# Turn of the hidden rows and down product, each one gate/up tile earlier in the steps of a mixture-of-experts loop

## The chip, the cores and the metric

The kernel runs on one core of a Trainium2 chip. The metric is the device time of one execution in microseconds (us); lower is better. TensorE multiplies matrices into accumulator banks, VectorE and ScalarE work on rows, GpSimd helps in the early stages, and SyncE (SP) issues most transfers. 16 DMA engines carry the data of the core.

## The reference

One decoder layer for 256 prompt rows and 8 sample rows, all in float32: projections, block-sparse attention, a memory attention, a short convolution, an output projection with LayerNorm, and then a mixture of experts with a second LayerNorm. The part that matters here is the mixture: each of the 264 rows goes to its top 4 of 32 experts.

```python
def expert_block(args):
    xb, e = args
    gu = xb @ w_gate_up[e] + b_gate_up[e]          # 1024 x 2048 weights
    g, u = jnp.split(gu, 2, axis=-1)
    g = jnp.minimum(g, SWIGLU_LIMIT)
    u = jnp.clip(u, -SWIGLU_LIMIT, SWIGLU_LIMIT)
    hid = (u + 1.0) * g * jax.nn.sigmoid(SWIGLU_ALPHA * g)
    return hid @ w_down[e] + b_down[e]             # 1024 x 1024 weights
```

The results are weighted by the router's softmax and summed per row.

## The kernel before

**Stages.** The first 340 us hold projections, attention, router and the making of a block table. From 341 us to about 1345 us the mixture runs; the last LayerNorm ends the kernel.

**Blocks and steps.** The rows of an expert are cut into blocks of 32 slots. With these inputs there are 51 blocks for 32 experts: 18 experts have one block, 10 have two, three have three and one has four (expert 5 is blocks 8 to 11, expert 6 is 12 to 14, expert 16 is 25 to 27, expert 23 is 37 to 39). Block i is worked on in step i of TensorE's loop (L952). A step multiplies the block's rows with eight gate/up tiles (`gate_up_tile`, L876), and in between does the second half of the block before it, d = i - 1: it turns that block's hidden rows (`turn_hidden`, L902, two transposes) and multiplies them with the four down tiles (`down`, L910). Odd steps (side 1) also gather the rows of the next pair of blocks after tile 4 and turn them after tile 5; even steps (side 0) instead add a finished pair into the sums after tile 5 (`add_pair`, L929).

**Weights.** One expert's weights are eight gate/up tiles and four down tiles of 1 MB each, and there is room for one expert only. SP's loop (L480) loads expert e: for each gate/up tile it waits until the last block of expert e - 1 has used it (`gu_used`, L483), issues the load, and then does the same with the four down tiles (`dn_used`, L487). All waits of SP stand in this one order, so a down tile's wait holds back the next expert's gate/up loads. TensorE waits for a gate/up tile at L878 and for a down tile at L920.

**Hidden rows.** After tile 7 VectorE takes four operations (`hidden`, L1819 to L1830) and ScalarE a sigmoid (L1203) to make the hidden rows of the block. `turn_hidden` waits for them (`hd_ready`, L904), ScalarE copies the turned rows (L1192), `down` waits for that copy (L912), and ScalarE copies its result (L1198). `down` first multiplies a bias row (L916), which releases VectorE's next bias row (`hot_used`).

**Expert numbers.** `pe.value_load` reads the number of the expert of block i (L960) and that of block d (L964) into registers; the waits at L878 and L920 use them.

Of the kernel before, what the change touches and what calls it, by code (L numbers as in the profile page):

```python
# [47 lines left out]
def layer_kernel(nc, x_prompt, x_sample, cache_k, cache_v, cache_mem_k, cache_mem_v, state_conv, page_table,  # L48
# [47 lines left out]
    with ctx:  # L96
# [405 lines left out]
        def _(pe):  # L502
# [343 lines left out]
            def gather(n):  # L846

                pe.wait_ge(hot_ready, n + 1)
                pe.wait_ge(rows_split, 1)
                for c in range(2):  # L850
                    for piece in range(3):
                        for half in range(2):
                            pe.matmul(p_gather[half * PAIR:(half + 1) * PAIR, :], slot_hot_b[:, c, :],  # L853
                                      x_pieces[c][piece][:, half * HALF:(half + 1) * HALF],
                                      start=(c == 0 and piece == 0), stop=False)
                for half in range(2):
                    last = pe.matmul(p_gather[half * PAIR:(half + 1) * PAIR, :], slot_hot_b[0:PACKED, 2, :],
                                     sample_packed[:, half * HALF:(half + 1) * HALF], start=False, stop=True)
                last.then_inc(gat_ready, 1)

            def turn_gathered(n):

                pe.wait_ge(gat_copied, n + 1)
                for j in range(4):
                    last = pe.transpose(p_gather[:, j * PARTS:(j + 1) * PARTS], xg[:, j * PARTS:(j + 1) * PARTS], ident[:, :])
                last.then_inc(xgt_ready, 1)

            def gate_up_bias(i, side):

                pe.wait_ge(bias_hot_ready, i + 1)  # L870
                for g in range(GROUPS):
                    pe.matmul(p_gu[side][g * SLOTS:(g + 1) * SLOTS, :], bias_hot[side].broadcast_to([3 * E, SLOTS]),
                              bias_up.rearrange("p (s n) -> p s n", s=2)[:, :, g * QUARTER:(g + 1) * QUARTER],
                              start=True, stop=False)

            def gate_up_tile(e, side, k):  # L876

                pe.wait_ge(gu_in[k], e * 16 + 16)  # L878
                for g in range(GROUPS):
                    last = pe.matmul(p_gu[side][g * SLOTS:(g + 1) * SLOTS, :],  # L880
                                     xg_t[:, k % 4, k // 4, side * SLOTS:(side + 1) * SLOTS],
                                     gate_up_w[:, k, :].rearrange("p (s n) -> p s n", s=2)[:, :, g * QUARTER:(g + 1) * QUARTER],
                                     start=False, stop=(k == KC - 1))
                last.then_inc(gu_used, 1)
# [17 lines left out]
            def turn_hidden(n):  # L902

                pe.wait_ge(hd_ready, n + 1)  # L904
                for r in range(2):
                    last = pe.transpose(p_hid_t[:, r * PARTS:(r + 1) * PARTS],  # L906
                                        hid.rearrange("p (c r) -> p r c", r=2)[:, r, :], ident[:, :])
                last.then_inc(hdt_ready, 1)

            def down(n, side, hot, e):  # L910

                pe.wait_ge(hdt_copied, n + 1)  # L912
                pe.wait_ge(dn_copied, 2 * n + 2)
                places = (0, PAIR) if side == 0 else (PAIR, 0)
                for h in range(2):
                    last = pe.matmul(p_down[places[h]:places[h] + SLOTS, :], hot.broadcast_to([3 * E, SLOTS]),  # L916
                                     bias_down[:, h * HALF:(h + 1) * HALF], start=True, stop=False)
                last.then_inc(hot_used, 1)
                for k in range(DK):
                    pe.wait_ge(dn_in[k], e * 16 + 16)  # L920
                    for h in range(2):
                        for r in range(2):
                            at_row = places[h] + r * SLOTS
                            last = pe.matmul(p_down[at_row:at_row + SLOTS, :], hid_t[:, r, k, :],  # L924
                                             down_rows[:, k, r, h * HALF:(h + 1) * HALF],
                                             start=(k == 0 and r == 1), stop=(k == DK - 1))
                    last.then_inc(dn_used, 1)

            def add_pair(pair, d, u):  # L929

                h, t = u // 4, u % 4
                if u == 0:
                    pe.wait_ge(weight_ready, pair + 1)
                if t == 0:
                    pe.wait_ge(dn_copied, 2 * d + (3 + h))
                pe.wait_ge(sum_added, 8 * pair + (u + 6))
                pe.matmul(bank[5 + u % 3][:, 0:T], pair_rows[:, h, t * PARTS:(t + 1) * PARTS], slot_weight_t[:, h, :],  # L937
                          start=True, stop=True).then_inc(sum_ready, 1)
# [13 lines left out]
            with pe.Fori(0, MAX_BLOCKS // 4) as group:  # L952
                for j, side in ((0, 1), (0, 0), (1, 1), (1, 0)):
                    q = group * 2 + j
                    i, d = group * 4 + (2 * j + 2 - side), group * 4 + (2 * j + 1 - side)
                    with pe.If(i < count):
                        pe.wait_ge(xgt_copied, i + 1)
                        pe.wait_ge(gu_read, i)
                        gate_up_bias(i, side)
                        e_up = pe.value_load(block_expert[0:1, bass.ds(i, 1)], min_val=0, max_val=E - 1)  # L960
                        for k in range(KC):
                            gate_up_tile(e_up, side, k)
                            if k == 1:
                                e_down = pe.value_load(block_expert[0:1, bass.ds(d, 1)], min_val=0, max_val=E - 1)  # L964
                            elif k == 2:
                                turn_hidden(d)
                            elif k == 3:
                                down(d, 1 - side, bias_hot[1 - side], e_down)
                            if side == 1:
                                if k == 4:  # L970
                                    gather(q + 1)
                                elif k == 5:
                                    turn_gathered(q + 1)
                            elif k == 5:
                                for u in range(8):
                                    add_pair(q, d, u)
                    with pe.Else():
                        pass
# [975 lines left out]
```

## Time and profile before

| | us |
|---|---|
| median of 3 runs | 1367.52 |
| range of the runs | 1364.51 to 1369.04 |
| the profiled execution | 1364.17 |
| its span on the core | 1362.4 |
| TensorE matmul busy | 1083.2 (80%) |
| VectorE busy | 612.0 (45%) |
| ScalarE busy | 231.4 (17%) |
| data moved | 499.39 MB, mean 367 GB/s |

Busy shares are averages over the span. TensorE's matmuls are pipelined and overlap in the records: the sum of their lengths is more than the time they take up, and the chain of waits shows the time that each adds. The releaser that a row names is the last one in the profile, which need not be what an engine stood for.

### The profile page before, as it was taken

The page shows a single profiled execution, that of the slowest core. Times are in us where ns is not written, and L with a number is a line of the kernel's source. Part 1 is how long each engine was busy: PE and PEld are TensorE (multiplying, and loading weights), DVE is VectorE, ACT ScalarE, POOL GpSimd, SP SyncE. Part 2 cuts the span into 40 slices and gives each one's busy share as a digit, 9 for nine tenths or more (in the row PEclk, how much of TensorE's full clock was granted, in tenths as well). Part 3 has the DMA queues.
Part 4 walks back from the last instruction along what each step waited for, and adds up shares of the span by engine and source line. Part 5 has one row for each costly group of instructions (what it writes and reads, how often), then busy time and mean ns, then how long its engine had stood idle before and what let it go on. Part 6 is the DMA issues. An engine that isn't in the chain of part 4 may idle for free.

```text
span 1362.4 us, 21271 instructions
## 1 busy us (share of the span) xinstructions
PE 1083.2 (80%) x7568; PEld 492.7 (36%) x7569; DVE 612.0 (45%) x1054; ACT 231.4 (17%) x505; POOL 154.9 (11%) x140
## 2 busy tenths in 40 slices
PE   7996757795997999976555569976969995869965
PEld 5775433232442344422212123422413441323423
DVE  1699865237644354533221215522534453324526
ACT  1211541113211111110000001211111111111112
POOL 2676722010600000000000000000000000000000
PEclk9999777897998999977877779977979997889988
DMA  9977949688899956699999999699999879999993
GB/s 368 374 309 286 397 156 366 267 316 335 362 409 421 422 237 272 260 421 422 421 422 421 422 423 421 270 422 422 422 422 421 367 324 422 422 422 421 423 422 132
DMA packets 72560, 499.39 MB, mean 367 GB/s; under 512 B 7459, under 2 KB 8022, under 8 KB 19190
## 3 DMA queue, kind: packets, MB, share of 16 engines
q1 hardware_dynamic: 66384, 430.14, 76.7%
q0 software_dynamic: 4816, 67.27, 12.4%
q10 hardware_dynamic: 1334, 1.64, 0.3%
q8 instruction: 16, 0.26, 0.1%
q14 instruction: 10, 0.08, 0.0%
HBM read 496.32 MB, written 2.71 MB: 366 GB/s over the span
## 4 chain that ended last, share of the span: by engine, by line
PE 45%; DMA 40%; DVE 7%; issue 4%; SPq 3%; POOL 1%; ACT 1%; ACTq 0%; DVEq 0%; POOLq 0%
DMA gate_up_w<-in_w_gate_up 23%; PE bank L880 15%; DMA down_w<-in_w_down 12%; PE bank L924 11%; PE bank L937 4%; PE bank L676 2%; PE bank L756 2%; DVE down_w L1484 2%; DMA gate_up_w<-in_w_out 2%; SPq L484 1%; PE bank L553 1%; DMA ring_b<-in_cache_k,page_row 1%; PE bank L906 1%; DMA ring_a<-in_cache_k,page_row 1%; PE bank L853 1%
## 5 line engine op out<-in xcount | busy, mean ns | idle before, releaser
L880 PE MATMUL bank<-gate_up_w,ring_b 128*32 128x512 f32 x3264 | 453.5, 654 | 178.0 <-DMA gate_up_w<-in_w_gate_up 177.7
L880 PEld LDWEIGHTS bank<-gate_up_w,ring_b 128*32 128x32 f32 x3264 | 102.0, 113 | 400.7 <-DMA gate_up_w<-in_w_gate_up 254.2
L924 PE MATMUL bank<-down_w,ring_b 128*32 128x512 f32 x1632 | 200.1, 598 | 10.5 <-DMA down_w<-in_w_down 10.5
L1812 DVE TENSOR_SCALAR work<-work 96x1 f32<-96x1 f32 x52 | 10.9, 209 | 325.4 <-PE bank L916 325.1
L1806 DVE TENSOR_TENSOR ring_a<-ring_a,bank 128x264 f32<-128x264 f32 x200 | 85.8, 429 | 138.7 <-PE bank L937 135.9
L924 PEld LDWEIGHTS bank<-down_w,ring_b 128*32 128x32 f32 x1632 | 89.3, 111 | 88.7 <-DMA down_w<-in_w_down 24.1
L1425 POOL TENSOR_TENSOR gate_up_w<-gate_up_w,ring_a 128x1024 f32<-128x1024 f32 x1 | 2.5, 2528 | 988.8 <-ACT gate_up_w L1238 988.8
L1198 ACT ACTIVATE ring_b<-bank 64x512 f32<-64x512 f32 x100 | 59.1, 591 | 240.2 <-PE bank L924 239.0
L937 PE MATMUL bank<-ring_b 128*128 128x264 f32 x400 | 95.7, 393 | 0.0
L937 PEld LDWEIGHTS bank<-ring_b 128*128 128x128 f32 x400 | 73.5, 189 | 32.8 <-issue 21.0
L1823 DVE TENSOR_SCALAR ring_b<-bank 128x256 f32<-128x256 f32 x51 | 21.6, 424 | 128.0 <-PE bank L880 128.0
L1192 ACT ACTIVATE ring_b<-bank 128x256 f32<-128x256 f32 x51 | 19.5, 383 | 336.7 <-PE bank L906 336.7
L1769 DVE SCALAR_TENSOR_TENSOR ring_a<-ring_a 128x1056 f32<-128x1056 f32 x50 | 66.7, 1334 | 0.9
L1772 DVE TENSOR_REDUCE ring_b<-ring_a 128x264 f32<-128x1056 f32 x50 | 62.6, 1253 | 1.7
L553 PE MATMUL bank<-x_cols,gate_up_w 128*128 128x264 f32 x256 | 61.0, 400 | 0.6 <-ACT x_cols L1043 0.6
L1203 ACT ACTIVATE ring_b<-ring_b 128x256 f32<-128x256 f32 x51 | 21.2, 416 | 223.8 <-DVE ring_b L1823 223.8
L553 PEld LDWEIGHTS bank<-x_cols,gate_up_w 128*128 128x128 f32 x256 | 49.9, 197 | 13.1 <-issue 2.3
L1484 DVE TENSOR_REDUCE down_w<-ring_b 128x32 f32<-128x2048 f32 x20 | 45.3, 2280 | 2.3 <-POOL ring_b L1322 2.1
L1478 DVE TENSOR_TENSOR ring_b<-ring_b,bank 128x2048 f32<-128x2048 f32 x12 | 27.3, 2279 | 38.3 <-ACT gate_up_w L1049 26.9
L1322 POOL TENSOR_TENSOR ring_b<-ring_b,gate_up_w 128x2048 f32<-128x2048 f32 x8 | 36.1, 4538 | 34.7 <-ACT gate_up_w L1049 26.7
L676 PE MATMUL bank<-gate_up_w,x_cols 128*128 128x512 f32 x64 | 30.6, 634 | 9.3 <-DMA gate_up_w<-in_w_out 9.3
L906 PEld LDWEIGHTS bank<-consts,ring_b 128*128 128x128 f32 x102 | 16.0, 206 | 57.1 <-issue 32.0
(367 smaller groups left out, 1082.1 us busy)
## 6 DMA issues: line engine op xcount, KB each, us to landing
gate_up_w<-in_w_gate_up SPq DMA_DIRECT2D x256, 1024.0 KB, 14.1
down_w<-in_w_down SPq DMA_DIRECT2D x128, 1024.0 KB, 11.4
gate_up_w<-in_w_in SPq DMA_DIRECT2D x4, 2048.0 KB, 19.7
gate_up_w<-in_w_out SPq DMA_DIRECT2D x1, 4096.0 KB, 23.9
ring_a<-in_w_in SPq DMA_DIRECT2D x1, 2048.0 KB, 24.9
ring_a<-in_w_mem_kv SPq DMA_DIRECT2D x1, 2048.0 KB, 28.1
gate_up_w<-in_cache_mem_k SPq DMA_DIRECT2D x1, 2048.0 KB, 15.3
gate_up_w<-in_cache_mem_v SPq DMA_DIRECT2D x1, 2048.0 KB, 20.3
```

The lines of the kernel that those rows point to most:

```text
L553: last = pe.matmul(out[:, 0:T], w, x_cols[:, k, :], start=(k == 0), stop=(k == KC - 1))
L676: last = pe.matmul(banks[half][0:rows, :], o_cols[:, j, c * PARTS:c * PARTS + rows], w_o[:, j, half * HALF:(half + 1) * HALF], start=(j == ...
L880: last = pe.matmul(p_gu[side][g * SLOTS:(g + 1) * SLOTS, :], xg_t[:, k % 4, k // 4, side * SLOTS:(side + 1) * SLOTS], gate_up_w[:, k, :].r ...
L906: last = pe.transpose(p_hid_t[:, r * PARTS:(r + 1) * PARTS], hid.rearrange("p (c r) -> p r c", r=2)[:, r, :], ident[:, :])
L924: last = pe.matmul(p_down[at_row:at_row + SLOTS, :], hid_t[:, r, k, :], down_rows[:, k, r, h * HALF:(h + 1) * HALF], start=(k == 0 and r = ...
L937: pe.matmul(bank[5 + u % 3][:, 0:T], pair_rows[:, h, t * PARTS:(t + 1) * PARTS], slot_weight_t[:, h, :], start=True, stop=True).then_inc(s ...
L1198: act.activation(pair_rows[at_row:at_row + PAIR, h, :], bank[1][at_row:at_row + PAIR, :], ACT.Copy)\
L1322: pool.tensor_tensor(pages, pages, q_wide[b % 4].unsqueeze(1).broadcast_to([PARTS, 4, AW]), ALU.mult)\
L1484: last = dve.tensor_reduce(scores[:, 4 * q:4 * q + 4, b * HEADS:(b + 1) * HEADS], page_quarter(b, q).rearrange("p (g h d) -> p g h d", g=4 ...
L1769: dve.scalar_tensor_tensor(weight_parts, token_slots, row_slots[:, h:h + 1], token_weights, ALU.is_equal, ALU.mult)\
L1772: return dve.tensor_reduce(slot_weight_t[:, h, :], weight_parts, AX.X, ALU.add)
L1806: dve.tensor_tensor(expert_sum[:, u, :], expert_sum[:, u, :], bank[5 + u % 3][:, 0:T], ALU.add)\
```

## The change

In each step the turn of the hidden rows moves from behind gate/up tile 2 to behind tile 1, the down product from behind tile 3 to behind tile 2, and the load of the down product's expert number from behind tile 1 to behind tile 0 (tiles are counted from 0). Nothing else is altered; what follows the last step (L979 on) stays as it is.

```diff
                         for k in range(KC):
                             gate_up_tile(e_up, side, k)
-                            if k == 1:
+                            if k == 0:
                                 e_down = pe.value_load(block_expert[0:1, bass.ds(d, 1)], min_val=0, max_val=E - 1)
+                            elif k == 1:
+                                turn_hidden(d)
                             elif k == 2:
-                                turn_hidden(d)
-                            elif k == 3:
                                 down(d, 1 - side, bias_hot[1 - side], e_down)
                             if side == 1:
                                 if k == 4:
```

## Rows read from the trace of the kernel before

**Rows 1.** Windows: stretch, its length, busy us (records) of each engine, TensorE clock, DMA share, GB/s

```profile
378.00:495.00 117.00, 104.22 (x836) 44.44 (x830) 49.73 (x102) 17.63 (x37) 0.00 (x0) 0.94 1.01 422
495.00:523.00 28.00, 27.45 (x230) 11.67 (x222) 14.90 (x30) 4.83 (x10) 0.00 (x0) 1.00 0.04 16
524.00:553.00 29.00, 29.00 (x250) 13.17 (x242) 14.90 (x30) 5.21 (x11) 0.00 (x0) 1.00 1.01 421
553.00:567.00 14.00, 14.00 (x130) 5.61 (x124) 9.29 (x15) 3.23 (x7) 0.00 (x0) 1.00 0.10 29
567.00:865.00 298.00, 205.50 (x1482) 76.65 (x1476) 89.98 (x183) 31.29 (x66) 0.00 (x0) 0.82 1.01 421
865.00:878.00 13.00, 12.61 (x98) 5.76 (x102) 5.04 (x12) 1.98 (x4) 0.00 (x0) 1.00 0.13 38
```

**Rows 2.** Chain of waits in a streaming stretch: start, us, what

```profile
608.74 3.51 PE bank L924 x29
615.77 20.93 DMA gate_up_w<-in_w_gate_up
638.01 3.50 PE bank L924 x30
```

**Rows 3.** Chain of waits around 498 us, where a gap begins

```profile
483.42 14.63 DMA down_w<-in_w_down
...
498.10 1.06 PE bank L924 x8
499.16 0.86 PE bank L880 x8
...
505.31 2.58 PE bank L880 x24
```

**Rows 4.** Timeline of TensorE: start, us, operation; idle time before it and what ended it

```profile
865.39 1.06 PE L924 MATMUL bank<-down_w,ring_b 128*32 128x512 f32 x8 [0.59 <-DMA down_w<-in_w_down]
1086.25 1.06 PE L924 MATMUL bank<-down_w,ring_b 128*32 128x512 f32 x8 [0.60 <-DMA down_w<-in_w_down]
```

**Rows 5.** Timeline of all engines in step 13: tiles 0 to 2, last hidden operation, turn

```profile
549.35 2.76 PE L880 MATMUL bank<-gate_up_w,ring_b 128*32 128x512 f32 x24
...
550.70 0.42 DVE L1830 TENSOR_TENSOR ring_b<-ring_b 128x256 f32<-128x256 f32 x1
...
552.03 0.31 PEld L906 LDWEIGHTS bank<-consts,ring_b 128*128 128x128 f32 x2 [0.84 <-DVE ring_b L1830]
```

**Rows 6.** Timeline: a VectorE result that TensorE stood waiting for

```profile
319.34 1.27 DVE L1587 SCALAR_TENSOR_TENSOR x_rows<-gate_up_w,small 8x1024 f32<-8x1024 f32 x1
...
320.66 0.57 PEld L688 LDWEIGHTS bank<-consts,x_rows 8*128 8x128 f32 x8 [0.78 <-DVE x_rows L1587]
```

**Rows 7.** Lines L960 and L964 in step 13: ends of the two register loads (ns, start us)

```profile
L960 PEldq SEQ_ASSERT  x1: 18/18/18, 549.0 to 549.0; - x1
L964 PEldq SEQ_ASSERT  x1: 18/18/18, 549.9 to 549.9; - x1
```

**Rows 8.** Timeline of SP: gate/up loads issued from step 11

```profile
521.58 2.04 SPq L484 DMA_DIRECT2D gate_up_w<-in_w_gate_up  x3
524.72 4.84 SPq L484 DMA_DIRECT2D gate_up_w<-in_w_gate_up  x2
```

**Rows 9.** Window: a hole in the stream in step 1

```profile
365.00:366.00 1.00, 1.00 (x15) 0.53 (x10) 1.00 (x1) 0.00 (x0) 0.03 (x1) 1.00 0.59 213
```

**Rows 10.** Chain of waits in the last step

```profile
1318.27 1.06 PE bank L880 x8
...
1319.54 3.45 PE bank L924 x32
1322.99 1.72 PE bank L880 x16
1324.70 3.76 PE bank L937 x16
```

**Rows 11.** Timeline: first gate/up tile of steps 6, 29 and 50 (of 16 such steps)

```profile
441.00 1.94 PE L880 MATMUL bank<-gate_up_w,ring_b 128*32 128x512 f32 x8 [9.89 <-DMA gate_up_w<-in_w_gate_up]
909.81 1.94 PE L880 MATMUL bank<-gate_up_w,ring_b 128*32 128x512 f32 x8 [6.80 <-DMA gate_up_w<-in_w_gate_up]
1310.80 1.94 PE L880 MATMUL bank<-gate_up_w,ring_b 128*32 128x512 f32 x8 [9.89 <-DMA gate_up_w<-in_w_gate_up]
```

## The prediction

> **What bounds the kernel now.** I read the page's slices first, then the windows, then the chain of waits, then single waits in the timeline.
>
> The windows split the expert part [rows 1] into two kinds of stretch. From 378 to 495, 524 to 553, 567 to 865 us and so on, the DMA engines are busy at a share of 1.01 and move 421 to 422 GB/s, whatever TensorE does (205.5 of 298 us busy in one of them). There the weight stream sets the time: 12 tiles per expert, each 1.049 MB / 422 GB/s = 2.48 us. In between lie four gaps in which almost nothing moves: 495 to 523, 553 to 567, 865 to 878, and 1086 to 1098 (not shown, same shape). These belong to the experts with three or four blocks (steps 8-11, 12-14, 25-27, 37-39): their weights stay in use until the last block, the next expert has nowhere to land, and TensorE is all but fully busy (27.45 of 28, 29.00 of 29, 14.00 of 14 us). So the run is: stream, plus gaps of TensorE work, plus a tail. Of the 51 steps, 16 wait 6.8 us or more for their first gate/up tile (first, shortest and last in [rows 11]); the other 35 run at TensorE's pace.
>
> The chain of waits in a streaming stretch [rows 2] reads "down product 3.5 us, then a gate/up transfer 20.9 us, then the down product": it looks as if every expert hung on the down product. It doesn't: that transfer is long because it queues behind others on busy DMA engines.
>
> How long a gap lasts is read from the chain at 498 us [rows 3]. The last down tile of the expert lands at 498.05; the last quarter of the down product (1.06 us), gate/up tile 4 (0.86 us), gather, tiles 5 to 7, the whole of step 10 and tile 0 of step 11 follow without a pause, and only then does SP issue the next gate/up tile, at 521.58 [rows 8]. The gaps at 865 and 1086 start the same way: TensorE stands 0.6 us before the last quarter of a down product until that tile lands [rows 4]. The gap at 553 has no landing in it: from 498 to 567 us TensorE waits for no transfer.
>
> **The change, part by part.** In each of 50 steps two transposes and the down product move ahead of one gate/up tile; the down product's four releases and SP's four down loads move with them, the load of the down product's expert number moves ahead of tile 1, and the release of tile 3 comes after the down product instead of before it. Nothing is added or removed. Steps of pure TensorE work keep their length if no new wait opens.
>
> 1. *Work behind the last landing.* In three gaps (498, 865, 1086) what lies between landing and release of the next expert's tile 0 is the path. The waiting instruction, the last quarter of the down product, has tile 3 in front of it now and behind it afterwards. One gate/up tile is 2.58 us / 3 = 0.86 us [rows 3]. The landing doesn't move, since the stream before it is full [rows 1]; TensorE just stands 0.6 + 0.86 us there. Cost 3 x 0.86 = **+2.6 us**. The gap at 553 is a chain of whole steps: no cost.
>
> 2. *Less cover for the turn.* The turn of the hidden rows starts at 552.03, behind tile 2 [rows 5]. Its input is done at 550.70 + 0.42 = 551.12. TensorE has loaded no weights for 0.84 us before it, but its matmuls run on: it waits for the array, not for VectorE, though the row names VectorE. Behind tile 1 it could start at 552.03 - 0.86 = 551.17. Another VectorE result (ends 320.61) let TensorE load at 320.66 [rows 6]: 0.05 us later. So the input is usable at 551.17 too: margin zero. No row shows this wait; its bounds are 0 and a whole tile, 0.86. It can't be below zero, because the array is busy until then. I take 0, by the nearest rows. Where it is on the path: between 498 and 564 us four turns (steps 10 to 13), none in the other two gaps. Sum 0, bounds 0 to +3.4 us. The copy of the turned rows keeps its cover: one tile lies between turn and product before and after.
>
> 3. *The expert number.* Its load ends at 549.9, that of the gate/up expert at 549.0 [rows 7], with tiles 0 and 1 handed out between. Handed out after tile 0 alone it ends about 549.8, while tile 1's matmul is due at 549.35 + 0.86 = 550.21. Hidden; 0 to 0.1 us in four steps.
>
> 4. *Tile 3 released late.* After a gap the stream starts from nothing, so each release counts. Tiles 0 to 2 feed it for 3 x 2.48 = 7.4 us, so tile 3 must be issued by 521.58 + 7.4 = 529.0. Before, the first tile behind the down product (tile 4) is issued at 529.2: two issues end at 524.72 + 4.84 = 529.56, and one takes 2.04 - 2 x 0.86 = 0.3 [rows 8]. Afterwards it is tile 3, one tile earlier, at 528.4. Margin 0.6 us, cost 0; if the start is ragged, up to 0.3 us in each of four gaps, **0 to +1.2**. Everywhere else down tiles queue ahead and cover it.
>
> 5. *Down tiles released earlier.* At full stream nothing is gained. The stream has small holes: at 365 us it drops to 213 of 422 GB/s for one microsecond [rows 9], because the first down reload is issued too late. The earlier product fills that, **-0.5 us at most**; the next gate/up loads are set by TensorE a few microseconds later, so I take 0.
>
> 6. *The tail.* In the last step tile 3 starts on its landing at 1318.27, product and tiles 4 and 5 follow, and the adds come at 1324.70 [rows 10]. Afterwards the product follows tile 2 and is over before tile 5 lands at 1318.27 + 2 x 2.48 = 1323.23; tile 5 takes 1.06 us like tile 3, and the adds come at 1324.3. **-0.4 us**.
>
> VectorE's and ScalarE's orders don't change; their work behind the product (bias row, slot weights, copies) only starts 0.86 us earlier.
>
> Of the clock: after 6.8 us or more of standing idle TensorE is granted the lower level, 1.2 GHz, and a tile takes 1.94 us [rows 11] instead of 1.06 [rows 10]. The product moves one tile nearer to those tiles and will run partly at 1.2 GHz in some of the 16 waiting steps. TensorE has over 6 us to spare there, so the sum doesn't change; only the last step could pay.
>
> The Trainium skill ("Perfetto Trace Analysis", Matmul Optimizations) says that the matmul engine scales its power with utilization and wants matmuls back to back in batches, which speaks against moving the product into a sparse stretch. By that rule the last step would pay up to a product's 3.45 us, by the rows nothing, since its tile 3 already ran in 1.06 us [rows 10].
>
> Sum: 2.6 + 0 + 0 + 0 + 0 - 0.4 = **+2.2 us**. The profiled execution took 1364.17 us (span 1362.4), which is 3.3 us under the median of the runs, 1367.52; so 1366.4 for an execution like it, and 1367.52 + 2.2 = **1369.7 us** for the median, +0.16%.
>
> **The rivals.**
> *The turn waits (slower).* If TensorE takes up a wait that isn't yet met later than 0.05 us, or the hidden rows come later, each turn at TensorE's pace costs w. Four lie on the path, and the two steps before each of the three landings first use up the 0.6 us of standing: total 2.2 + 4w + 3 x (2w - 0.6), the last term from w = 0.3 on. It passes 0.3% (4.1 us, about what a measurement of this kernel can tell from no change) from w = 0.37; at w = 0.5 it is +5.4 (1372.9), at w = 0.86 it is +9.0 (1376.5). For it: zero margin. Against: the 0.05 us of rows 6.
>
> *The chain is right (faster).* If the down reload's issue set the pace, as rows 2 read, it would come a tile landing (2.48 us) earlier in each of the 16 waiting steps: -40 us, 1328. Against it: a DMA share of 1.01 there leaves nothing to fill.
> The Trainium skill ("Perfetto Trace Analysis", Optimization Strategy) advises to find what the saturated engine waits for and make those dependencies start sooner, which is this rival's reasoning. It also gives 425 GB/s for large transfers and 435 for the fabric ("DMA: Bandwidth & Descriptors", Bandwidth); the trace's 422 agrees with a stream that is full.
>
> *Nothing moves (no change).* If the tile behind the landing is absorbed, because the stream recovers it from its own small holes, the time stays at 1367.5.
>
> **How the numbers follow.** Forecast 0.62, turn waits 0.20, nothing 0.12, chain right 0.06. The forecast lies 1.9 us below the 0.3% bound, and the three runs of before spread over 4.5 us, so 0.1 of its 0.62 would be measured as slower. Faster 0.06; same 0.52 + 0.12 = 0.64; slower 0.20 + 0.10 = 0.30. Range: below, the stream's holes filled and the spread of a median, 1365.5; above, late tiles of point 4 and w up to 0.6, about 1375.5. Outside are the chain rival and the far end of the turn's.
>
> **What would show it.** The waits before the last quarter of the down product near 498, 865 and 1086 us grow from 0.6 to 1.4 us, and the idle DMA stretches at the first, third and fourth gap each grow by 0.86 us, while the second keeps its length. The turn stands at 551.2 in a step like this one with hardly any TensorE idle time before it; if the waits list shows TensorE waiting for VectorE's last hidden operation in some 30 steps, the first rival holds. A DMA share under 0.95 within the first 10 us after a gap would mean point 4 was too kind. I am wrong if the streaming stretches move more than 422 GB/s, or if a gap changes by something other than one tile.

## The result and the profile after

| | before | after |
|---|---|---|
| median | 1364.83 us (20 runs, 1360.43 to 1382.15) | 1371.04 us (20 runs, 1366.86 to 1377.10) |
| ratio after / before | | 1.0039 (95% interval 1.0025 to 1.0054) |
| profiled execution, its span | 1364.17, 1362.4 us | 1371.56, 1369.8 us |

The change costs 0.39%, some 5.3 us. The ratio and its interval are of the fast runs alone, which leaves out one run of before (1382.15 us), and they are not the ratio of the two medians, which would be 1.0045. Timed a second time on another occasion it came to 1.0031 (1.0011 to 1.0050). The forecast was +2.2 us (+0.16%, range 1365.5 to 1375.5 us): the side of zero was right, the size was less than half of the 5.3 us. The absolute figure, 1369.7 us, lies only 1.3 us under the measured median, but by luck: it started from a median of three runs, 1367.52 us, which was 2.7 us above that of twenty. From 1364.83 us the same sum gives 1367.0 us, 4.0 us too low.

The windows after, cut where its stream stops and starts (columns as in rows 1):

```profile
378.00:495.00 117.00, 103.29 (x820) 43.92 (x816) 48.69 (x102) 16.85 (x35) 0.00 (x0) 0.94 1.01 420
499.00:525.00 26.00, 26.00 (x220) 12.33 (x216) 13.83 (x27) 4.84 (x10) 0.00 (x0) 1.00 0.00 0
528.00:556.00 28.00, 28.00 (x238) 13.02 (x233) 14.41 (x28) 5.22 (x11) 0.00 (x0) 1.00 1.00 406
559.00:569.00 10.00, 10.00 (x92) 3.26 (x88) 5.55 (x9) 2.86 (x6) 0.00 (x0) 1.00 0.04 7
572.00:869.00 297.00, 200.24 (x1460) 77.56 (x1452) 89.36 (x180) 31.33 (x66) 0.00 (x0) 0.82 1.01 420
870.00:882.00 12.00, 11.85 (x90) 5.40 (x94) 5.04 (x12) 1.78 (x4) 0.00 (x0) 1.00 0.04 5
```

The picture is that of [rows 1]: a full stream, and gaps in it while TensorE works. New is the third line: 406 GB/s after a gap, where [rows 1] had 421.

**A ruler for the stretches.** The early stages scatter: in thirteen profiles the first step starts anywhere from 337.2 to 344.0 us, though their code is the same in all. So I compare times inside the expert part, from one tile landing that TensorE waits for to another. These are the first gate/up tiles of steps 6, 16 and 29 after (timeline of TensorE); before they start at 441.00 and 909.81 [rows 11], and the middle one at 599.48.

```profile
442.66 1.94 PE L880 MATMUL bank<-gate_up_w,ring_b 128*32 128x512 f32 x8 [9.25 <-DMA gate_up_w<-in_w_gate_up]
604.11 1.94 PE L880 MATMUL bank<-gate_up_w,ring_b 128*32 128x512 f32 x8 [8.27 <-DMA gate_up_w<-in_w_gate_up]
917.28 1.08 PE L880 MATMUL bank<-gate_up_w,ring_b 128*32 128x512 f32 x4 [8.64 <-DMA gate_up_w<-in_w_gate_up]
```

With the first tiles of steps 41 and 50 (1139.36 and 1318.30 us after) and the end of the span this gives, in us, for the thirteen profiles:

| kernel | 6 to 16 (two gaps) | 16 to 29 (one) | 29 to 41 (one) | 41 to 50 (none) | 50 to the end | sum |
|---|---|---|---|---|---|---|
| before | 158.48 | 310.33 | 222.04 | 178.95 | 51.60 | 921.40 |
| before, again | 158.30 | 310.26 | 220.97 | 179.08 | 52.10 | 920.71 |
| the change | 161.45 | 313.17 | 222.08 | 178.94 | 51.50 | 927.14 |
| the change, again | 159.93 | 313.50 | 223.05 | 178.91 | 51.43 | 926.82 |
| turn only | 158.52 | 310.39 | 220.96 | 179.05 | 51.78 | 920.70 |
| tile 3 issued late | 160.34 | 311.91 | 221.38 | 178.90 | 51.71 | 924.24 |
| tile 3 issued later still | 160.75 | 313.19 | 224.11 | 179.06 | 51.52 | 928.63 |
| last quarter back | 158.30 | 310.26 | 221.04 | 178.90 | 51.57 | 920.07 |
| last quarter back, again | 158.28 | 310.54 | 221.06 | 178.98 | 50.86 | 919.72 |
| all one tile later | 159.42 | 309.46 | 220.14 | 179.11 | 53.45 | 921.58 |
| last quarter later | 158.32 | 309.58 | 219.91 | 179.08 | 52.76 | 919.65 |
| both splits | 158.46 | 309.58 | 220.26 | 179.11 | 52.51 | 919.92 |
| turn behind tile 0 | 165.21 | 313.30 | 224.87 | 178.86 | 52.10 | 934.34 |

The stretch without a gap is 178.9 to 179.1 us in every one of them, whatever TensorE's order: there the stream alone counts. Everything that the change costs lies in stretches with a gap, +1.5 to +3.1, +2.8 to +3.2 and, against 221.0, +1.1 to +2.1 us. The sums are 6.1 to 6.4 us above the repeat of before, and 5.4 to 5.7 us above its first profile. (The 222.04 of that first profile is its only value before step 50 that the second doesn't repeat; its restart at 1096 us took 1.2 us longer than the one in the repeat. That is chance, and about as large as some of the differences below.)

### The profile page after: what moved, and what is told of

Read it like the earlier page. It is cut to its first block, busy times and chain, and to the rows that moved or that the text cites. A ratio compares the mean times of both kernels' runs of the same rounds, so it can differ in the third digit from the quotient of the medians.

```text
span 1369.8 us, 21271 instructions
## 1 busy us (share of the span) xinstructions
PE 1083.0 (79%) x7568; PEld 502.0 (37%) x7569; DVE 611.3 (45%) x1054; ACT 231.7 (17%) x505; POOL 156.2 (11%) x140
## 3 DMA queue, kind: packets, MB, share of 16 engines
q0 software_dynamic: 4816, 67.27, 12.3%
## 4 chain that ended last, share of the span: by engine, by line
PE 47%; DMA 39%; DVE 6%; issue 4%; SPq 2%; POOL 1%; ACT 1%; DVEq 0%; ACTq 0%; POOLq 0%
DMA gate_up_w<-in_w_gate_up 22%; PE bank L880 16%; DMA down_w<-in_w_down 12%; PE bank L924 11%; PE bank L937 4%; PE bank L553 2%; PE bank L676 2%; PE bank L756 2%; DMA gate_up_w<-in_w_out 2%; DVE down_w L1484 2%; DMA ring_b<-in_cache_k,page_row 1%; PE bank L906 1%; DMA ring_a<-in_cache_k,page_row 1%; PE bank L853 1%; SPq L484 1%
## 5 line engine op out<-in xcount | busy, mean ns | idle before, releaser
L880 PE MATMUL bank<-gate_up_w,ring_b 128*32 128x512 f32 x3264 | 444.4, 643 | 182.9 <-DMA gate_up_w<-in_w_gate_up 182.6
L880 PEld LDWEIGHTS bank<-gate_up_w,ring_b 128*32 128x32 f32 x3264 | 108.6, 113 | 386.6 <-DMA gate_up_w<-in_w_gate_up 244.0
L924 PE MATMUL bank<-down_w,ring_b 128*32 128x512 f32 x1632 | 203.1, 603 | 15.4 <-DMA down_w<-in_w_down 15.4
## 6 DMA issues: line engine op xcount, KB each, us to landing
down_w<-in_w_down SPq DMA_DIRECT2D x128, 1024.0 KB, 12.5
gate_up_w<-in_w_out SPq DMA_DIRECT2D x1, 4096.0 KB, 23.5
ring_a<-in_w_in SPq DMA_DIRECT2D x1, 2048.0 KB, 25.8
```

Source lines behind the costliest of these rows:

```text
L880: last = pe.matmul(p_gu[side][g * SLOTS:(g + 1) * SLOTS, :], xg_t[:, k % 4, k // 4, side * SLOTS:(side + 1) * SLOTS], gate_up_w[:, k, :].r ...
```

## Where the time went

**One tile behind the last landing.** The chain after, at the third gap:

```profile
856.81 13.30 DMA down_w<-in_w_down
870.15 1.06 PE bank L924 x8
871.21 2.58 PE bank L880 x24
873.79 3.76 PE bank L937 x16
...
879.62 1.72 PE bank L880 x16
```

Behind the last down tile there are now three gate/up tiles (2.58 us) before the adds. From this landing, 870.11, to SP's issue of the next tile 0 at 880.7 are 10.6 us. Before it was 9.7 (865.34 to 875.1; below). The difference is the 0.86 us of the forecast. TensorE's standing before it did not grow to 1.4 us, as I had written (timeline of TensorE; [rows 4]):

```profile
870.15 1.06 PE L924 MATMUL bank<-down_w,ring_b 128*32 128x512 f32 x8 [0.59 <-DMA down_w<-in_w_down]
1093.77 1.06 PE L924 MATMUL bank<-down_w,ring_b 128*32 128x512 f32 x8 [0.59 <-DMA down_w<-in_w_down]
```

The tile that stands behind the landing one step pair earlier (24) had already made TensorE 0.86 us later, and the product came 0.86 us earlier in its step. The two cancel. Waits of 1.4 us stand elsewhere, in steps behind a streaming stretch (step 24 for one), before as after; the change puts a second wait in front of them (below).

**The restart.** I then followed the gate/up tiles that refill the buffer after this gap. SP's line L484 in narrow windows (last number of the first line: time of issue), with the time from issue to landing. First tiles 0, 3 and 7 before:

```profile
L484 SPq DMA_DIRECT2D gate_up_w<-in_w_gate_up x1: 337/337/337, 875.1 to 875.1; - x1
DMA to landing us min/median/max: 4.9/4.9/4.9
...
L484 SPq DMA_DIRECT2D gate_up_w<-in_w_gate_up x1: 333/333/333, 878.2 to 878.2; - x1
DMA to landing us min/median/max: 9.2/9.2/9.2
...
L484 SPq DMA_DIRECT2D gate_up_w<-in_w_gate_up x1: 333/333/333, 887.8 to 887.8; - x1
DMA to landing us min/median/max: 9.5/9.5/9.5
```

and after:

```profile
L484 SPq DMA_DIRECT2D gate_up_w<-in_w_gate_up x1: 336/336/336, 880.7 to 880.7; - x1
DMA to landing us min/median/max: 4.9/4.9/4.9
...
L484 SPq DMA_DIRECT2D gate_up_w<-in_w_gate_up x1: 333/333/333, 887.5 to 887.5; - x1
DMA to landing us min/median/max: 7.4/7.4/7.4
...
L484 SPq DMA_DIRECT2D gate_up_w<-in_w_gate_up x1: 333/333/333, 893.4 to 893.4; - x1
DMA to landing us min/median/max: 11.4/11.4/11.4
```

Tile 3 is issued 3.1 us behind tile 0 before, and 6.8 us after, as forecast to the tenth. But it lands 14.2 us behind tile 0's issue instead of 12.3, and tile 7, issued 12.7 us behind tile 0 in both, lands after 24.1 instead of 22.2 us. The restart has lost 1.9 us. The hole can be seen in the stream, in the microsecond from 9.0 to 10.0 us behind tile 0's issue and over the three from 9.3 to 12.3, before and after (windows, columns as in [rows 1]):

```profile
884.06:885.06 1.00, 1.00 (x10) 0.16 (x8) 0.22 (x2) 0.60 (x1) 0.00 (x0) 1.00 0.93 393
884.40:887.40 3.00, 3.00 (x28) 0.95 (x24) 0.00 (x0) 0.77 (x2) 0.00 (x0) 1.00 1.03 434
889.68:890.68 1.00, 1.00 (x10) 0.16 (x8) 0.00 (x0) 0.60 (x1) 0.00 (x0) 1.00 0.68 262
890.00:893.00 3.00, 3.00 (x28) 0.95 (x24) 0.00 (x0) 0.80 (x2) 0.00 (x0) 1.00 0.87 303
```

With an early tile 3 (before, its repeat, last quarter back) the restarts take 22.1 to 22.4 us at the first, third and fourth gap and 22.4 to 22.6 us at the second, but for one of 23.5 in the first profile of before. In the two profiles of the change the four take 23.7, 23.7, 24.1, 22.6 and 23.9, 23.1, 23.7, 23.5 us. The first restart doesn't count, since the gap behind it is a chain of TensorE's steps. The other three lost 3.5 and 3.4 us together.

**The clock.** A third cost stands between landing and issue. The times from the last landing to the next tile 0, in us:

| | first gap | third | fourth |
|---|---|---|---|
| before and its repeat | 23.5 | 9.7 | 9.7 |
| the change | 25.3 | 10.6 | 10.6 |
| the change, again | 24.4 | 11.2 | 10.7 |

Four of the six cells of the change are one tile longer, or within 0.13 us of it. The 25.3 and the 11.2 are longer by another 0.95 and 0.62 us. The chain says why. In the first profile it doesn't rest on the last landing at the first gap (499.72 us), but goes back from there through TensorE's own work to a landing two steps earlier, in step 7, behind which the clock was at its lower level, 1.2 GHz (the window in the experiment below); the second profile, where the clock stayed up, rests on the last landing there:

```profile
470.00 1.80 PE bank L924 x8
471.80 2.68 PE bank L880 x16
...
498.33 3.45 PE bank L924 x32
```

```profile
482.60 14.64 DMA down_w<-in_w_down
...
497.29 1.06 PE bank L924 x8
```

The quarter and the two tiles took 1.80 and 2.68 us instead of 1.06 and 1.72. TensorE came late by 1.7 us. Of these 0.55 were taken out of its standing before the last quarter, and 0.2 came back because a quarter takes 0.86 us in a running product and 1.06 behind a wait; 0.95 us were on the path. In the second profile the clock falls in step 24 instead, and in step 34, and there the chains at the third and fourth gap don't rest on the last landing. So the lower clock cost 0.95 us in one profile and 0.62 + 0.13 = 0.75 us in the other.

**The sum.** Against the repeat of before, the three stretches with a gap are longer by 7.2 us in the first profile of the change and by 6.9 us in the second. Of these, 3 x 0.86 = 2.6 us stand behind landings, 3.5 and 3.4 us at restarts, and 0.95 and 0.75 us are the clock's: 7.0 and 6.7 us. The two other stretches are 0.7 and 0.8 us shorter than in that repeat, mostly the last one, which leaves the 6.4 and 6.1 us of the table. The timed runs give 4.2 to 5.3 us with intervals that reach from 1.5 to 7.4.

## The experiments

**The change again** (no edit).

> The changed kernel again, beside the variants. Theory S (work behind the last landing plus a starved restart): +4 to +7 us against the kernel before; the down tile that lands last in front of each of the gaps at about 870 and 1094 us is waited for 0.6 us with the product ahead of tile 3, and DMA engines dip below a share of 0.95 some 8 to 10 us after the stream restarts. Theory C (the clock): the profile of the change had 1.2 GHz from 470.9 to 474.3 us, behind 0.45 and 1.41 us of standing inside one down product, which cost 1 to 1.7 us; if that is a property of the order it comes again at the same place, if it is chance it does not.

Measured: 1369.51 us, ratio 1.0031 (1.0011 to 1.0050); stretches in the table. The sign and the size are those of theory S, and the stream dips where it said, to 238 GB/s from 9.0 to 10.0 us behind the third restart. But the waits of 0.6 us at about 870 and 1094 us are gone in this profile: TensorE came late to both landings, behind falls of the clock in steps 24 and 34. The clock: in the first profile TensorE stood twice within one down product of step 7 and then ran at the lower level, 1.2 GHz (timeline of TensorE, and a window with a mean clock of 0.57):

```profile
467.52 1.07 PE L924 MATMUL bank<-down_w,ring_b 128*32 128x512 f32 x8 [0.45 <-DMA down_w<-in_w_down]
470.00 1.80 PE L924 MATMUL bank<-down_w,ring_b 128*32 128x512 f32 x8 [1.41 <-DMA down_w<-in_w_down]
471.56 2.92 PE L880 MATMUL bank<-gate_up_w,ring_b 128*32 128x512 f32 x16
```

```profile
471.00:474.00 3.00, 3.00 (x20) 0.64 (x12) 0.41 (x2) 1.18 (x2) 0.00 (x0) 0.57 1.01 421
```

In the second profile step 7 waits 0.44 and 1.41 us in just the same way and keeps its clock; instead the clock falls in steps 24 and 34, again behind two waits within one product, in step 24 these:

```profile
833.94 1.06 PE L924 MATMUL bank<-down_w,ring_b 128*32 128x512 f32 x8 [0.88 <-DMA down_w<-in_w_down]
836.42 1.94 PE L924 MATMUL bank<-down_w,ring_b 128*32 128x512 f32 x8 [1.42 <-DMA down_w<-in_w_down]
```

So the order brings double waits, six in each of the two profiles, and three of the twelve are followed by the lower level, at places that change from execution to execution. Theory C came out as neither of its two forms: the fall isn't tied to one place, but it comes with the order. It accounts for 0.95 of the 1.5 us by which the stretch from 6 to 16 differs between the profiles (161.45 and 159.93), and the second restart for another 0.7. No experiment takes the double waits out of the change.

**Turn only.**

```diff
-                            if k == 1:
+                            if k == 0:
                                 e_down = pe.value_load(...)
-                            elif k == 2:
+                            elif k == 1:
                                 turn_hidden(d)
```

> Only the turn and the expert number move one tile ahead; the down product stays behind tile 3. Theory S: 0.0 us (within 0.3%), the turn starts 2.05 us after the bias matmul of its step instead of 2.91. Rival T (the turn's lost cover is the cost): +4 to +5 us, as much as the whole change, and TensorE waiting for the last hidden operation in the waits list.

Measured: 1364.80 us, ratio 1.0011 (0.9986 to 1.0037), and the stretches of before, each within 0.1 us of one of its two profiles. The waits list has no wait of TensorE's matmuls for the hidden rows; for tiles it reads (total us, times, longest)

```profile
PE bank L880 <- DMA gate_up_w<-in_w_gate_up: 178.2, 57, 11.2
PE bank L924 <- DMA down_w<-in_w_down: 8.4, 10, 1.4
```

The turn and the expert number are free. The whole cost belongs to the down product's move.

**Tile 3 issued late.** TensorE's order is that of before.

```diff
-                    sp.wait_ge(gu_used, last * KC + (k + 1))
+                    sp.wait_ge(gu_used, last * KC + (5 if k == 3 else k + 1))
```

> The kernel before, but SP issues the reload of gate/up tile 3 only once tile 4 has been used, that is behind the down product; TensorE's order is untouched. It isolates the late release of tile 3 (0.86 us later even than in the change). Theory S: holes in the stream 8 to 10 us after each restart, 1 to 2 us each; the one at 523 us is swallowed by the next gap, three count: +3 to +6 us. Rival L (only the tile behind the last landing costs): 0.0 us.

Measured: 1365.02 us, ratio 1.0011 (0.9976 to 1.0046), too wide to tell. The stretches tell: +2.0, +1.6 and +0.4 us against the repeat of before, none where there is no gap. At the third gap tile 3 is issued 7.6 us behind tile 0 (at 874.8):

```profile
L484 SPq DMA_DIRECT2D gate_up_w<-in_w_gate_up x1: 333/333/333, 882.4 to 882.4; - x1
DMA to landing us min/median/max: 6.1/6.1/6.1
```

It lands at +13.7 us instead of +12.3, tile 7 at +23.6 instead of +22.2. The expert part is 3.5 us longer, within the 3 to 6 us expected and as much as the change's restarts, with no TensorE instruction moved.

**Tile 3 issued later still**, behind tile 5 (`6 if k == 3`).

> The kernel before, with tile 3's reload issued only once tile 5 has been used: a second dose of the late issue (behind tile 4 the stretch from step 16 to step 29 rose from 310.33 to 311.91 us). In odd steps the gather comes between tiles 4 and 5, so tile 3 is issued 2.8 us later than with the first dose. Theory S: the stretches from step 16 to 29 and from 29 to 41, whose gaps end in odd steps, rise by a further 2 to 3 us each, and the stretch without a gap stays at 178.9; the kernel +5 to +8 us. Rival L: 0.

Measured: 1372.60 us, ratio 1.0066 (1.0038 to 1.0094), some 9 us, and 7.9 us in the sum of stretches. The second dose adds 1.3 and 2.7 us to the stretches 16 to 29 and 29 to 41, less than the 2 to 3 us each that I expected in one of the two, and nothing to the stretch without a gap. At the third gap tile 3 is issued 10.3 us behind tile 0 (at 878.8):

```profile
L484 SPq DMA_DIRECT2D gate_up_w<-in_w_gate_up x1: 333/333/333, 889.1 to 889.1; - x1
DMA to landing us min/median/max: 4.7/4.7/4.7
```

4.7 us is also what the very first tile of a restart takes (4.7 to 5.0): tile 2 had landed 9.9 us behind tile 0's issue, so nothing was in flight any more.

**Last quarter back.** The change, but the fourth down tile's product behind gate/up tile 3 again. (The diff shows the calls; `down` now takes the numbers of its down tiles, and waits and multiplies the bias row only with the first of them.)

```diff
                             elif k == 2:
-                                down(d, 1 - side, bias_hot[1 - side], e_down)
+                                down(d, 1 - side, bias_hot[1 - side], e_down, (0, 1, 2))
+                            elif k == 3:
+                                down(d, 1 - side, bias_hot[1 - side], e_down, (3,))
```

> The change with one part undone: only the last quarter of the down product (the fourth down tile) goes back behind gate/up tile 3; the first three quarters stay behind tile 2. It takes the extra tile from behind the last landing and leaves most of the late release of tile 3. Theory S: the stretch from the first gate/up landing of step 16 to that of step 29 (one gap; 310.33 us before, 313.2 and 313.5 in the two profiles of the change) comes to about 312.0, 1.3 us above before and 0.9 or more below the change; the whole kernel +1 to +3 us. Rival L (only the landing costs): 310.4 and no difference to before. Rival R (only the late release costs): 313.

Measured: 1361.68 us, ratio 0.9975 (0.9953 to 0.9997), and 310.26 us from step 16 to 29: no stretch is longer than before. I had expected 312.0, with most of the late release left. What I had overlooked is that tile 3 now comes one quarter (0.9 us) sooner, 5.9 us behind tile 0 (at 876.6):

```profile
L484 SPq DMA_DIRECT2D gate_up_w<-in_w_gate_up x1: 333/333/333, 882.5 to 882.5; - x1
DMA to landing us min/median/max: 6.2/6.2/6.2
```

It lands at +12.1, in time. So this edit undoes the landing's tile and the late release at once and cannot tell them apart; its stretch of 310.3 happens to be what rival L foretold, but the two experiments on SP contradict that rival. Three quarters of the product can move for nothing; all of the cost, 6 us, comes with the fourth.

**Last quarter back, again** (same kernel).

> The change with only the last quarter of the down product behind tile 3, once more, because its first timing (0.9975, interval 0.9953 to 0.9997) was below that of before while its profiled stretches were the same (158.3, 310.3, 221.0). If the stretches are right: 1.000 within 0.002. If the timing is right: 0.9975 again, and the gain lies before the first step.

Measured: 1367.00 us, ratio 1.0017 (0.9992 to 1.0042). The stretches were right, the 0.9975 did not come again, and nothing shows a difference between this kernel and before.

**Before, again** (no edit, one execution).

> The kernel before once more, for the spread of the stretches between profiles of one program: 158.5, 310.3, 222.0, 178.9 us between the first landings of steps 6, 16, 29, 41 and 50. If restarts are exact, each comes again within 0.2 us; if the landing of tiles behind a restart has a spread of its own, the three that hold a gap differ by up to 1 us and the one without a gap does not.

Measured: 158.30, 310.26, 220.97, 179.08 us, 1362.1 us for the one execution. Three stretches come again within 0.2 us, the one from 29 to 41 (222.04 in the first profile) 1.07 us lower.

**All one tile later.** Turn behind tile 3, product behind tile 4, adds behind tile 6.

> The opposite direction: turn behind tile 3, down product behind tile 4, adds behind tile 6. Theory S: 3 x 0.86 = 2.6 us less behind the last landings, against up to 0.9 us for a first down reload that comes later, 0.4 us at the restart after the second gap and up to 1.5 us in the last step: -2.6 to +0.5 us. If the order is symmetric (each tile earlier costs 5 us, each tile later gives 5 us) it would be -5 us.

Measured: 1364.54 us, ratio 1.0006 (0.9986 to 1.0026). The two single gaps give back 0.80 and 0.83 us against the repeat, one tile each as expected; from landing to issue they last 8.9 us instead of 9.7. The stretch with two gaps loses 1.1 us, and the last one 1.4 to 1.9 us, probably because the last step's product now stands behind a later tile. Earlier costs, later gains nothing: not symmetric.

**Last quarter later.** Before, with the fourth down tile's product behind tile 4 and the adds behind tile 6 (the diff leaves out the adds' line and the same change of `down`).

```diff
                             elif k == 3:
-                                down(d, 1 - side, bias_hot[1 - side], e_down)
+                                down(d, 1 - side, bias_hot[1 - side], e_down, (0, 1, 2))
+                            elif k == 4:
+                                down(d, 1 - side, bias_hot[1 - side], e_down, (3,))
```

> The kernel before with its turn and three quarters of the down product in place, but the last quarter behind tile 4 and the adds behind tile 6. It takes one tile (0.86 us) from behind each last landing and leaves the release of tile 3 alone. Theory S: the stretches with a gap shorten by 0.86 us each, -2.0 to -2.6 us in all, the tail unchanged. Rival L gives the same. Rival R: 0.

Measured: 1363.22 us, ratio 0.9994 (0.9971 to 1.0016). The single gaps shorten by 0.68 and 1.06 us, the stretch with two gaps by nothing, and the last stretch is 0.7 us longer: -1.1 us in the sum of stretches against the repeat of before, where -2.0 to -2.6 us were expected, and too little for the timed runs.

**Both splits.** Turn and three quarters as in the change, last quarter behind tile 4, adds behind tile 6.

> Turn behind tile 1 and three quarters of the down product behind tile 2 as in the change, the last quarter behind tile 4, the adds behind tile 6. Tile 3 is released 5.9 us after tile 0, which was early enough with the last quarter behind tile 3; one tile less stands behind each last landing. Expected of both theories: the stretches with a gap 0.7 to 1.1 us under those of before (309.5 and 219.9), -2 us in all; if tile 3 at 5.9 us is at the edge after all, the landing of tile 3 comes more than 2.6 us behind that of tile 2.

Measured: 1362.64 us, ratio 0.9996 (0.9978 to 1.0014), stretches as in the kernel above. Apart from the 0.9975 that did not come again, no variant beats before by more than its interval.

**Turn behind tile 0.** Before, with only the turn moved, two tiles ahead.

```diff
-                            if k == 1:
+                            if k == 0:
+                                turn_hidden(d)
+                            elif k == 1:
                                 e_down = pe.value_load(...)
-                            elif k == 2:
-                                turn_hidden(d)
```

> The kernel before with only the turn moved two tiles ahead, behind tile 0. It measures the wait that the prediction bounded by 0 and 0.86 us per step. If the hidden rows are just in time behind tile 1, TensorE now stands 0.86 us (one tile) before the turn in each step of its own pace, and waits for the last hidden operation some 35 times, about 30 us in all; of that 4 x 0.86 and 3 x (0.86 x 2 - 0.6) = 6.8 us are on the path, the rest is taken up by transfers. If the rows were ready well before tile 1 ends, the wait is shorter by that margin and the kernel less slow.

Measured: 1378.49 us, ratio 1.0116 (1.0093 to 1.0140). The waits list has the wait at last (total, times, longest):

```profile
PE bank L906 <- DVE ring_b L1830: 25.8, 33, 0.8
```

25.8 / 33 = 0.78 us a time, not 0.86: behind tile 1 the rows are ready 0.08 us before the array is free. The number of waits was right, the part of them on the path was not: the expert part is 13.6 us longer and not 6.8. I had let the landings of down tiles take up the waits between gaps, but with 0.78 us more in every step TensorE no longer stands for a down tile in steps 9, 26, 36 and 38. From the last landing in front of a gap to tile 0 of the refill it takes 8.6 us more in all, counting the first two gaps as one chain. Another 4.1 us lie behind the refills at the third and fourth gap, which I had left out: from the landing of their tile 7 to the first tile of the next expert it takes 14.5 us instead of 12.5.

## Why the prediction was right or wrong

The forecast mechanism, one tile behind each last landing, held and had its size right. The sum was too small by 3.1 us on the timed ratio (5.3) and by 4 us on the stretches (6.1 to 6.4), because two other terms were put at zero: the late tile 3 (3.5 us) and the clock (0.95 and 0.75 us).

1. *Work behind the last landing, +2.6 us:* right. Landing to issue grew from 9.7 to 10.6 us at the third gap, and moving the last quarter the other way gives back 0.7 to 1.1 us a gap. Wrong in the sign I named for it: the standing stays at 0.59 us, or vanishes where the clock fell before. That "a gap changes by something other than one tile" was to be a sign of being wrong, and at the first gap of the first profile it did, by 1.8 us; the clock is the difference.

2. *Less cover for the turn, 0:* right. The same places after, in step 13 (timeline; [rows 5]):

```profile
552.83 1.90 PE L880 MATMUL bank<-gate_up_w,ring_b 128*32 128x512 f32 x16
...
554.19 0.42 DVE L1830 TENSOR_TENSOR ring_b<-ring_b 128x256 f32<-128x256 f32 x1
...
554.67 0.31 PEld L906 LDWEIGHTS bank<-consts,ring_b 128*128 128x128 f32 x2 [0.84 <-DVE ring_b L1830]
```

The turn starts 2.06 us behind the bias matmul of its step (552.61) instead of 2.90, a tile earlier, 0.06 us behind the end of its input, and TensorE's matmuls run through. The row still names VectorE and still shows 0.84 us, as it did with a tile more of cover. The first rival fell with this, and the experiment with the turn behind tile 0 shows what it would have looked like.

3. *The expert number, 0:* right, by the turn-only kernel.

4. *Tile 3 released late, 0 of 0 to +1.2:* **the step that failed.** The times of issue were right to 0.1 us. The limit was not: I let tile 3 be issued until tiles 0 to 2 have run for 7.4 us, which takes for granted that a tile in flight behind others lands one transfer time after them, however late it was issued. In the change tile 3 takes 7.0 and 7.4 us from issue to landing at this gap, where 5.5 us were left (12.3 - 6.8). With 5.9 us the restart is whole, with 6.8 us it loses 0.4 to 1.9 us, with 7.6 us it loses 1.4 us at this gap. Each restart that counts lost 1.2 us on average where the range allowed 0.3. This term is 3.5 of the 7 us that the stretches with a gap lost. The sign that I had named came: a DMA share under 0.95 within 10 us of the restart (0.68 above; the same microsecond of before has 0.93, so the bound was set too close). Why a tile issued at 6.8 us takes so long the runs don't show.

5. *Down tiles released earlier, 0 (at most -0.5):* not settled. The hole of [rows 9] is worth less than the scatter of its stretch: the time from the first step to the first landing in step 6 is 99.5 and 101.8 us in its two profiles and 100.3 and 100.9 us in those of before.

6. *The tail, -0.4 us:* not seen. The last stretch is 51.5 us after and 51.6 and 52.1 before. In the chain of the last step after (compare [rows 10]) the product runs partly at the lower clock and takes 4.15 instead of 3.45 us, so the adds come 14.06 us behind the first landing (1318.30) instead of 13.90:

```profile
1325.63 4.15 PE bank L924 x32
1329.78 2.58 PE bank L880 x24
1332.36 3.76 PE bank L937 x16
```

The Trainium skill wants matmuls back to back ("Perfetto Trace Analysis", Matmul Optimizations), and this row agrees with it, by 0.7 us and not by the 3.45 us that I had worked out for it.

7. *The clock, 0 outside the last step:* also wrong, and smaller. I had looked at the product behind the 16 long waits, where TensorE has time to spare, and that costs nothing indeed. What I missed is that the new order makes TensorE stand twice within one product in the step behind some of them, 0.4 to 0.9 us and then 1.2 to 1.4 us, and that the clock can fall there; in steps 7, 24 and 34 TensorE's own work runs on from there to a gap.

The second rival, a gain from earlier reloads of the down tiles, fell: the stretch without a gap is the same within 0.3 us in all kernels. The chain of waits [rows 2] names the down product there, and moving it does nothing. The third, no change, fell by the interval.

The two larger causes, landing and release, were never separated inside the change itself, because any order that puts the last quarter ahead of tile 3 also delays tile 3's release. They were separated beside it: the release by the two experiments on SP's waits, the landing by the times from landing to issue and by the kernels that move the last quarter the other way. The clock's part is read from the chains alone.

## What to carry to other kernels

Where a buffer is refilled in single copy, look at two intervals per refill rather than at busy shares: from the last landing to the first release, which is pure path, and from the first release to the release that comes behind the longest piece of other work. A producer-consumer order that is free in the steady stream can cost at each restart, and an early instruction is no gain if what it is moved ahead of is a release. And compare terms and not only totals: the first two causes here add up to 6.1 us, the same as a total over all stretches, only because that total also holds a gain of 0.8 us in stretches that they don't touch.

## What the runs showed of the hardware

A transfer of 1.049 MB into an idle set of queues took 4.7 to 5.0 us from issue to landing, in a stream that lands one every 2.48 us. In these runs a stream that had only three tiles queued had to be fed a fourth before the three had run out: issued 5.9 us behind the first it landed on time, issued 6.8 us behind it 1.5 to 1.9 us late at the third gap (0.4 to 1.6 us at the others), although the three last 7.4 us. The stream then fell to 262 of 422 GB/s for a microsecond. Why tile 3 took 7.0 to 7.4 us in the change and 6.1 us when issued later still, at 7.6 us, the runs don't show.

The clock fell to 1.2 GHz behind two waits of 0.4 to 1.4 us within one product in three of the twelve such places of the change's two profiles, where TensorE was otherwise busy, and in step 7 it stayed up in the second profile behind the same two waits that it had fallen behind in the first. In the two profiles of before no product has two waits, and the clock stays up behind single waits of 1.4 us. A fall made a quarter of the down product and the tiles behind it 1.5 to 1.7 us longer; 0.95 us of that showed at the first gap, 0.62 at the third and 0.13 at the fourth.
